# A blocked transpose on VectorE in the inverse of a gated delta rule, and a start that normalizes x tile by tile

## What is computed

```python
h = rmsnorm(x, attn_norm[i])
proj = h @ w_in[i]
qa, ka, va, qb, kb, vb, zb, bb, ab, gl = jnp.split(proj, cuts, axis=-1)
...
# gated delta rule, chunks of 64 tokens
A = jnp.eye(C) + jnp.where(strict, kkT * decay, 0.0)
sol = lax.linalg.triangular_solve(A, rhs, left_side=True, lower=True, unit_diagonal=True)
```

## Time and profile before

| what | value |
|---|---|
| median of 3 runs | 1338.13 us (1337.78 to 1340.0) |
| profiled execution | 1338.62 us |
| its span, first to last instruction | 1336.6 us |
| TensorE busy, share of the span | 1269.8 us, 95% |
| VectorE | 705.7 us, 53% |
| ScalarE | 516.8 us, 39% |
| GpSimd | 634.0 us, 47% |
| time of the first scores, of turn 0, of turn 7 | 62.35, 121.93, about 628 us |

### The profile page before, as it was taken

How to read it: one execution, slowest core, us unless ns; L and a number is a source line. 1 busy time by engine, 2 the same in 40 slices (tenths; PEclk the granted TensorE clock), 3 DMA queues, 4 the chain that set the end, 5 groups by cost and what they waited for, 6 DMA issues and landing times.

```text
span 1336.6 us, 21408 instructions
## 1 busy us (share of the span) xinstructions
PE 1269.8 (95%) x7509; PEld 989.0 (74%) x7509; DVE 705.7 (53%) x1154; ACT 516.8 (39%) x819; POOL 634.0 (47%) x757
## 2 busy tenths in 40 slices
PE   4889999999999999999999999999999999999998
PEld 3657777777777776776788888878887778888776
DVE  3353738475564748376522123118888852871633
ACT  4343544545354544546314222452422122222252
POOL 2433343342434343332544646347666784575543
PEclk9989999999999999999999999999999999999999
DMA  6412111121211111120222435223333242333222
GB/s 186 116 44 63 49 48 49 48 59 38 64 47 49 49 51 46 48 64 21 60 70 73 111 90 168 72 64 92 97 95 94 83 121 80 94 84 104 62 78 82
DMA packets 188136, 100.64 MB, mean 75 GB/s; under 512 B 3654, under 2 KB 186905, under 8 KB 188057
## 3 DMA queue, kind: packets, MB, share of 16 engines
q1 hardware_dynamic: 188057, 99.59, 26.3%
HBM read 97.47 MB, written 2.11 MB: 75 GB/s over the span
## 4 chain that ended last, share of the span: by engine, by line
PE 45%; POOL 20%; issue 18%; DVE 9%; ACT 5%; SPq 1%; DMA 0%; POOLq 0%; DVEq 0%; ACTq 0%
PE bank L496 30%; POOL w_lo L432 20%; PE bank L607 1%; PE bank L692 1%; PE bank L617 1%; PE bank L573 1%; PE bank L593 1%; PE bank L696 1%; PE bank L680 1%; DVE ast L1336 1%; ACT silu L986 1%; DVE qb L1362 1%; ACT silu L987 1%; ACT pr L968 1%; DVE o_b L1417 1%
## 5 line engine op out<-in xcount | busy, mean ns | idle before, releaser
L432 POOL TENSOR_TENSOR w_lo<-w_raw,w_hi 128x256 fp32r<-128x256 f32 x692 | 569.4, 856 | 303.2 <-ACT w_hi L895 298.3
L496 PE MATMUL bank<-hn_hi,w_hi 128*128 128x512 f32 x1000 | 425.3, 425 | 9.8 <-POOL w_lo L432 9.7
L496 PE MATMUL bank<-hn_hi,w_lo 128*128 128x512 f32 x1000 | 393.8, 394 | 0.0
L496 PE MATMUL bank<-hn_lo,w_hi 128*128 128x512 f32 x1000 | 393.0, 393 | 0.0
L446 POOL CAST w_hi<-w_raw 128x1024 fp32r<-128x1024 f32 x61 | 64.4, 1056 | 382.9 <-PE bank L496 382.9
L496 PEld LDWEIGHTS bank<-hn_hi,w_hi 128*128 128x128 f32 x1000 | 189.5, 190 | 61.6 <-issue 19.6
L496 PEld LDWEIGHTS bank<-hn_hi,w_lo 128*128 128x128 f32 x1000 | 189.1, 189 | 41.2
L496 PEld LDWEIGHTS bank<-hn_lo,w_hi 128*128 128x128 f32 x1000 | 190.0, 190 | 38.0 <-issue 6.7
L895 ACT ACTIVATE w_hi<-w_raw 128x1024 fp32r<-128x1024 f32 x120 | 127.5, 1062 | 109.5 <-PE bank L496 95.5
L1197 ACT ACTIVATE s<-u 128x512 f32<-128x512 f32 x22 | 13.9, 634 | 178.4 <-DVEq L1633 178.4
L1630 DVE SCALAR_TENSOR_TENSOR u<-vr,pt,u 128x511 f32<-128x511 f32 x88 | 74.8, 850 | 12.9 <-DVE u L1628 1.2
(11 more groups left out here) (269 smaller groups left out, 1861.8 us busy)
## 6 DMA issues: line engine op xcount, KB each, us to landing
w_raw<-in_w_in SPq DMA_DIRECT2D x73, 512.0 KB, 3.8
w_raw<-in_w_up SPq DMA_DIRECT2D x44, 512.0 KB, 3.8
w_raw<-in_w_down SPq DMA_DIRECT2D x16, 512.0 KB, 3.9
w_raw<-in_w_br_a SPq DMA_DIRECT2D x8, 512.0 KB, 3.8
w_raw<-in_w_br_b SPq DMA_DIRECT2D x8, 512.0 KB, 4.0
w_raw<-in_w_out SPq DMA_DIRECT2D x8, 512.0 KB, 4.1
w_raw<-in_w_ple_gate SPq DMA_DIRECT2D x8, 512.0 KB, 4.0
w_raw<-in_w_down SPq DMA_DIRECT2D x8, 384.0 KB, 3.5
```

The source lines that it names most:

```text
L432: ins = pool.tensor_tensor(wlo[c.slot][:, ks, :], raw[c.slot][:, ks, :], whi[c.slot][:, ks, :].bitcast(F32), ALU.subtract)
L496: mm = pe.matmul(acc, w[c.slot][:, i, :], xx[:, x0 + i, :], start=(i == 0 and n == 0), stop=last)
```

## The change

In the turns, VectorE makes `xi` after level 0, and `xt` after the levels 1 to 4, by transposing the other one in blocks of 32x32 in place (an instruction of VectorE). Up to level 4 all blocks of X off the 32x32 diagonal are zero, so this equals the full transpose. The product at line 657 and the third product of the levels 1 to 4 go, and `level_vt` is signalled by the second product there. Level 5 keeps its third product, level 6 is as it was.

At the start, ScalarE's queue issues the 13 parameter loads; SP's queue issues x, constants, the ba weight, the two loads for the bias line, the qa weight, three small loads, ka and va, and the lead turn's weights after `slope`. Each tile of x gets its own logarithm, exponential and scaling; TensorE transposes six channel blocks tile by tile into six banks, then the last two. TensorE's bias products move ahead of qa, the sums of squares of qa and ka one chunk earlier each. All high halves of the early weights are made by GpSimd. `STEPS_LEAD` changes, with four steps ahead of the first scores.

```diff
-STEPS_LEAD = ((8, 1, 1, 1, 2), (1,) * 6, (1, 1, 1, 1, 1, 1), (2, (1, 1), (1, 1), (1, 1), (1, 1)), (4, 6))
+STEPS_LEAD = (4, (5, 1, 1, 1, 2), (2, 1, 3, 2, 2, 2), (2, 0, 2, 0, 2, 0), (2, (1, 1), (1, 1), (1, 1), (1, 1)), (0, 1))
...
-        IN_BANKS = (3, 4, 5, 1, 2)
+        IN_BANKS = (3, 4, 5, 1, 2, 7)
...
@@ sync @@
-            for plane, row, src in rows:
-                sp.dma_start(prow[row:row + src.shape[0], plane, :], src).then_inc(sem("params_in"), 16)
...
+            load(stream.ba.at(0), w_in0, COLS["ba"])
+            sp.dma_start(hot[:, :], consts[0:33, C_HOT * P:]).then_inc(sem("lines_in"), 16)
+            sp.dma_start(tab[0:32, :], rel_bias).then_inc(sem("lines_in"), 16)
+            load(stream.first.at(0), w_in0, COLS["qa"])
...
+            for n, name in enumerate(("ka", "va")):
+                load(stream.first.at(1 + n), w_in0, COLS[name])
             sp.wait_ge(sem("line_ready"), 1)
...
+            for n, name in enumerate(LEAD):
+                load(stream.lead.at(n), w_in0, COLS[name] + (AHEAD[name] - 1) * P)
@@ gpsimd @@
-            for c in [stream.ba.at(0)] + [stream.first.at(n) for n in range(3)] + [stream.lead.at(n) for n in range(3)]:
-                split(c)
-            for n in range(3, 6):
-                both(stream.lead.at(n))
+            for c in [stream.ba.at(0)] + [stream.first.at(n) for n in range(3)] + [stream.lead.at(n) for n in range(6)]:
+                both(c)
@@ tensor @@
-            pe.wait_ge(sem("small_in"), 16 * 5)
...
+            pe.wait_ge(sem("lines_in"), 16 * 2)
+            pe.wait_ge(sem("tab_set"), 1)
             pe.matmul(bank[6][0:H, 0:LINE], tab[:, :], hot[:, :], start=True, stop=True).then_inc(sem("line_mm"), 1)
...
+            pe.wait_ge(sem("pt_ready"), 1)
+            for t in range(NT):
+                pe.wait_ge(sem("x_normed"), t + 1)
+                for c in range(len(IN_BANKS)):
+                    mm = pe.transpose(bank[IN_BANKS[c]][:, t * P:(t + 1) * P], x_tok[:, t, c * P:(c + 1) * P], ident)
...
             run(gemm(stream.ba.at(0), hn_hi, hn_lo, ready=("h_split", 0)))
-            run(gemm(stream.first.at(0), hn_hi, hn_lo), gemm(stream.first.at(1), hn_hi, hn_lo))
...
             pe.wait_ge(sem("slope_in"), 16)
...
+            run(gemm(stream.first.at(0), hn_hi, hn_lo))
...
+            run(gemm(stream.first.at(1), hn_hi, hn_lo))
...
+            qk_sum(0, 0, stream.first.at(0))
             run(gemm(stream.first.at(2), hn_hi, hn_lo))
+            qk_sum(0, 1, stream.first.at(1))
...
-                if delta:
-                    pe.wait_ge(sem("ct"), h * (NL - 1) + 1)
-                    for t in range(NT):
-                        for q in (LOW, UP):
-                            mm = pe.matmul(packed(7, 0, t, q), ct[0][q, t, :], ident2[q, :], start=True, stop=True)
-                    mm.then_inc(sem("c1"), 1)
...
                         for t in range(NT if n < NL - 1 else 0):
                             for q in (LOW, UP):
-                                pe.matmul(packed(5, 0, t, q), xt[q, t, :], ui[q, t, :], start=True, stop=True)
-                        for t in range(NT):
+                                mm = pe.matmul(packed(5, 0, t, q), xt[q, t, :], ui[q, t, :], start=True, stop=True)
+                        for t in range(NT if n >= NL - 2 else 0):
@@ scalar @@
+            for plane, row, src in rows:
+                act.dma_start(prow[row:row + src.shape[0], plane, :], src).then_inc(sem("params_in"), 16)
...
+                done(nc.scalar.activation(lnx[:, t:t + 1], ss0[:, t:t + 1], ACT.Ln, bias=sm[:, 28:29], scale=1.0 / D),
+                     "x_ln", t + 1)
+                done(nc.scalar.activation(rs0[:, t:t + 1], lnx[:, t:t + 1], ACT.Exp, scale=-0.5), "x_r", t + 1)
...
-                if c == 4:
-                    high(stream.ba.at(0))
...
@@ vector @@
+            def scaled(t):
+                dve.wait_ge(sem("x_r"), t + 1)
                 done(V.tensor_scalar(x_tok[:, t, :], x_tok[:, t, :], rs0[:, t:t + 1], None, ALU.mult), "x_normed", t + 1)
+
+            scaled(0)
+            scaled(1)
             dve.wait_ge(sem("params_T"), 1)
...
             done(V.tensor_copy(line[:, :], bank[6][0:H, 0:LINE]), "line_ready", 1)
+            scaled(2)
+            scaled(3)
...
+                    done(V.transpose(flat(xi), flat(xt)), "xi", h * (NL - 1) + 1)
                 if attention:
                     combine(a, 0)
                 if delta:
-                    dve.wait_ge(sem("c1"), h + 1)
-                    done(V.tensor_tensor(xi[:, :, :], ident2.unsqueeze(1).to_broadcast([P, NT, HEAD]), packed(7),
-                                         ALU.subtract), "xi", h * (NL - 1) + 1)
...
-                            done(V.tensor_tensor(xt[:, :, :], xt[:, :, :], packed(5, 1), ALU.subtract),
-                                 "xt", h * NL + (n + 1))
+                            if n < NL - 2:
+                                done(V.transpose(flat(xt), flat(xi)), "xt", h * NL + (n + 1))
+                            else:
+                                done(V.tensor_tensor(xt[:, :, :], xt[:, :, :], packed(5, 1), ALU.subtract),
+                                     "xt", h * NL + (n + 1))
```

More of the change, by code:

```diff
@@ L373, in _ @@
             sp.dma_start(slope[:, :, :], skew).then_inc(sem("slope_in"), 16)
-            for n, name in enumerate(LEAD[3:]):
-                load(stream.lead.at(3 + n), w_in0, COLS[name] + (AHEAD[name] - 1) * P)
+            for n, name in enumerate(LEAD):
+                load(stream.lead.at(n), w_in0, COLS[name] + (AHEAD[name] - 1) * P)
             for h in range(H - 2):
@@ L562, in _, with qk_sum @@
                           start=True, stop=True).then_inc(sem("bias_mm"), 1)
+            run(gemm(stream.first.at(0), hn_hi, hn_lo))
+            pe.wait_ge(sem("ba_copied"), 1)
+            for t in range(NT):
+                mm = pe.transpose(bank[5][:, t * 16:t * 16 + 16], ba_sb[:, t * P:(t + 1) * P], ident[0:16, 0:16])
+            mm.then_inc(sem("ba_T"), 1)
+            run(gemm(stream.first.at(1), hn_hi, hn_lo))
+            def qk_sum(h, n, c):
+                pe.wait_ge(sem("a_sq"), h * 2 + (n + 1))
+                pe.matmul(bank[c.bank][:, :], half, sqr[n][:, :], start=True, stop=True).then_inc(sem("a_sum"), 1)
+            qk_sum(0, 0, stream.first.at(0))
             run(gemm(stream.first.at(2), hn_hi, hn_lo))
+            qk_sum(0, 1, stream.first.at(1))
             pe.wait_ge(sem("g_ready"), 1)
@@ L568, in _ @@
             pe.matmul(bank[5][:, 96:128], ones, gg, start=True, stop=True).then_inc(sem("g_sums"), 1)
-            def qk_sum(h, n, c):
-                pe.wait_ge(sem("a_sq"), h * 2 + (n + 1))
-                pe.matmul(bank[c.bank][:, :], half, sqr[n][:, :], start=True, stop=True).then_inc(sem("a_sum"), 1)
             def v_turn(h):
@@ L631, in turn @@
                 f = Fill(*fill)
-                early, first, second, scan, late = steps
+                early, first, second, scan, late = steps[-5:]
+                if len(steps) > 5:
+                    f.step(steps[0])
                 if attention:
@@ L938, in v_copy @@
                 done(nc.scalar.activation(va[:, :], bank[4][:, :], ACT.Copy), "va_ready", h + 1)
-            for c in (stream.first.at(0), stream.first.at(1), stream.first.at(2)):
-                high(c)
+            act.wait_ge(sem("lam_sum"), 1)
+            done(nc.scalar.activation(lam_s, lam_s, ACT.Exp), "lam_exp", 1)
+            done(nc.scalar.activation(alexp, alog[:, :], ACT.Exp), "a_exp0", 1)
             prep_qk(0, 0, stream.first.at(0))
-            high(stream.lead.at(0))
             def plane(n):
@@ L952, in _ @@
             prep_qk(0, 1, stream.first.at(1))
-            high(stream.lead.at(1))
+            prep_r(0, 0, stream.first.at(0))
             prep_v(0, stream.first.at(2))
-            high(stream.lead.at(2))
             act.wait_ge(sem("g_cum"), 1)
@@ L1292, in _ @@
             dve.sem_inc(bank_free[c.bank], 1)
+            for n in range(H // 2):
+                bias_copy(n)
             dve.wait_ge(sem("ba_T"), 1)
@@ L1298, in _ @@
                                  dtb[:, :].unsqueeze(1).to_broadcast([P, NT, H]), ALU.add), "ba_planes", 2)
-            for n in range(H // 2):
-                dve.wait_ge(sem("bias_mm"), n + 1)
-                done(V.tensor_copy(bias[:, 2 * n:2 * n + 2, :].rearrange("p a b -> p (a b)"), bank[6 + n % 2][:, :]),
-                     "bias_ready", n + 1)
             dve.wait_ge(sem("soft"), 3)
```

77 lines of the change are left out of this document (28 added, 49 removed).

## The result

The change takes the time from 1338.5 us (1337.78 to 1340.0, 4 runs) to 1307.09 us (1306.03 to 1308.72, 4 runs): ratio 0.9765, 95% interval 0.9748 to 0.9782. Forecast was 1303, range 1294 to 1316. The profiled execution took 1306.31, its span is 1304.5, so 32.1 less than the span of before.

The account below looks back on a forecast made before the run. TensorE, busy 95%, was taken as the bound, shared with VectorE between the first and fifth xi of a middle turn. Gains of 20 us before turn 0 and 14.9 in the turns took 1338.1 to 1303 us, range 1294 to 1316.

Parts of the forecast that it names:

- TensorE's share, 2.79 per turn: Inverse levels on TensorE alone: removed products save 0.71 plus 4 x 0.52, 2.79 us per turn, 22.3 for 8 turns.
- The transpose, 0.42: VectorE in the inverse levels: each 128x256 transpose takes 0.42 us, like the update it replaces; 0.3 and 0.84 kept as alternatives.
- Rival 3: VectorE's transpose in the levels costs 0.84 us, middle turns gain 1.0 instead of 1.8: 1309 us, chance 0.11.
- rival 4: Slower: a very long VectorE transpose delays operations queued behind it, deciding from 1.7 us; at 2.0, 1348 us; chance 0.03.
- Middle turns, 1.8 each: Turns 0 to 5: 1.27 us up to level 4's product plus 0.52 after it, 1.8 each, 10.8 in all.
- rival 1: VectorE has more room, contended rows could relax, turns gain TensorE's whole share of 22.3 us: 1296 us, chance 0.12.
- Turn 0, 1.8: First full turn after the lead turn, counted among turns 0 to 5 as gaining 1.8 us like a middle turn.
- Turn 6, 1.3: Turn without filling in the second half of its levels: gains VectorE's 1.23 us, say 1.3.
- Nothing downstream gives it back: After the turns, from 700 us on, TensorE does matrix products back to back, so the turns' 14.9 us stay gained.
- The start, 20: Everything before turn 0: first scores at 51.5, turn 0 at 101.5 instead of 121.93 us, 20.4 gained, taken as 20.
- Rival 2: Start gains only 10 to 12 us: bias line and slope late on SP's queue, or ba slow-clocked; 1312 us, chance 0.20.
- The lead turn, 50: Turn before turn 0: 43.6 us of work, 5.5 idle and 1 for the clock, 50 in place of 59.58.

Follow-up runs that it names:

- the inverse part alone: Kernel before with only the blocked transposes in place of the inverse levels' products, its start, weights and step lists unchanged: 1322.53 us, ratio 0.9883.
- the start alone: Kernel after with the product behind level 0 and the third products put back, new start and lead-turn list kept: 1320.89 us, ratio 0.9871.
- the identity product back: Kernel after with the ident2 product after level 0 and the xi update from its bank restored in place of the first transpose: 1313.51 us, ratio 0.9814.
- gate and norm later: Kernel after with the previous head's o_b and following VectorE operations moved from behind the third side step to behind the seventh: 1304.89 us, ratio 0.9748.

## Why the prediction held, and where its terms were off

**What bounds the kernel, and the mechanism: right.** VectorE's unbroken stream between the first and the third `xi` passes on what TensorE saves ahead of it and swallows what TensorE saves beside it. Doubling the transposes and putting one product back each moved the time as that picture says.

**TensorE's share, 2.79 per turn: right.** Turn 7, the only one with VectorE nearly free, gained 2.69.

**The transpose, 0.42: measured 0.445.** Rival 3's 0.84 and rival 4's 1.7 are out. From the two-byte figure of the Trainium skill ("VectorE: DVE Perf Modes", "The three transpose paths") the forecast had worked out an estimate of 0.44; the trace agrees with it, for a four-byte tile of 128x256.

**Middle turns, 1.8 each: measured 2.2; the wait, 1.3: measured 0.78.** The term that was off is that the third product's removal doesn't shorten VectorE's stream, and it was put at nothing. The first `xi` of turn 1 came forward by 1.26 counted from the scores (1.23 forecast), but from there to the third `xi` VectorE took 11.04 in place of 11.51. The 0.47 are almost all `o_b`: 0.87 in place of 1.38. This is where GpSimd's copy stands in the three kernels (start and duration), with `o_b` under it; before, after, doubled transposes:

```profile
293.38 1.04 POOL L446 CAST w_hi<-w_raw 128x1024 fp32r<-128x1024 f32 x1 [6.65 <-PE bank L496]
293.59 1.38 DVE L1417 TENSOR_TENSOR o_b<-o_b,sqo 128x512 f32<-128x512 f32 x1
```

```profile
197.25 1.04 POOL L428 CAST w_hi<-w_raw 128x1024 fp32r<-128x1024 f32 x1 [5.71 <-PE bank L476]
197.96 0.87 DVE L1412 TENSOR_TENSOR o_b<-o_b,sqo 128x512 f32<-128x512 f32 x1
```

```profile
198.36 1.04 POOL L428 CAST w_hi<-w_raw 128x1024 fp32r<-128x1024 f32 x1 [5.70 <-PE bank L476]
200.03 0.73 DVE L1412 TENSOR_TENSOR o_b<-o_b,sqo 128x512 f32<-128x512 f32 x1
```

In the first two `o_b` ends 0.69, its undisturbed duration, after a moment 0.14 or 0.15 ahead of the copy's recorded end; in the third the copy was over. The Trainium skill ("SBUF — State Buffer", "SBUF: two separate sides") says that VectorE's operations with two SBUF inputs and GpSimd's share a port pair that one of them holds for its whole instruction while the other stands still. The trace agrees here: 1.38 and 0.87 are "wait, then 0.69". It was not tested by an experiment of its own; the three starts above are what shows it. Forward 1.26, plus 0.47, plus the fourth third product's 0.52, is 2.25 against 2.2 measured. The forecast named this as rival 1's "for" and then kept the contended duration as a constant.

**Turn 0, 1.8: measured 3.8.** The window of before:

```profile
121.93:196.86 74.93, 73.25 (x562) 54.93 (x562) 43.40 (x87) 33.94 (x66) 26.75 (x34) 0.98 0.17 46
```

A granted clock of 0.98, where turn 1 has 1.00: behind a wait of 1.77 at its first scores, filling matmuls took 0.63 from 123.8 to 126.4. After, that wait is 0.26 and the clock 1.00. The two experiments split it: with the inverse part alone turn 0 takes 72.74, 2.2 less, like every middle turn; with the start alone 73.31, 1.6 less. So 1.6 us that this turn gained belong to the start and its clock. The forecast had counted turn 0 as one more middle turn and had nothing for this: a gain by luck, which hides part of the start's shortfall.

**Turn 6, 1.3: measured 0.** VectorE's first `xi` of the levels came 1.25 earlier, as forecast. Then the contention that eased the middle turns went the other way: the product with `silu` met GpSimd's subtraction, and only 0.80 of the 1.25 reached the product of level 4. In before and in after:

```profile
595.11 0.69 DVE L1377 TENSOR_TENSOR qb<-qb,silu 128x512 f32<-128x512 f32 x1
```

```profile
563.12 1.10 DVE L1372 TENSOR_TENSOR qb<-qb,silu 128x512 f32<-128x512 f32 x1
...
570.19 0.42 DVE L1455 TENSOR_TENSOR xi<-xi,bank 128x256 f32<-128x256 f32 x1 [1.17 <-PE bank L670]
```

TensorE's wait grew from 1.7 to 2.78, and the lower clock behind it took the 0.80: VectorE's next `xi` waited 1.17 for TensorE, where it had waited for nothing in before, and both kernels pass the second sum of squares within 0.04 of each other, counted from the scores. The forecast had no term for the clock behind a longer wait. Moving filling there gave 3.6 back.

**Nothing downstream gives back: not quite.** 1.4 came back between 945 and 1211, where TensorE waits for GpSimd's low halves 8.6 us in 11 waits against 7.4 in 10. The stretch before and after:

```profile
979.09:1243.14 264.05, 256.67 (x1122) 208.77 (x1120) 168.64 (x209) 61.73 (x65) 173.81 (x191) 1.00 0.33 94
```

```profile
945.55:1211.06 265.51, 256.90 (x1121) 208.81 (x1120) 168.89 (x209) 61.65 (x65) 174.21 (x191) 1.00 0.32 93
```

The code there is the same in all kernels. Between the same two products it takes 264.0 with the start alone, with doubled transposes and with the identity product back, 264.8 with the inverse alone, and 265.4 to 265.5 in after and the eight other runs. So neither part of the change alone brings the 1.4. What makes one or the other come stays open.

**The start, 20: measured 16.** First scores at 54.36, not 51.5; 2.3 of the 2.9 are ba's end (27.3, not 25). Step by step: the two loads for the bias line landed at 13.1 as assumed (13). The two tiles behind the line copy took 2.28, not 1.6, beside GpSimd's early halves (1.54 with GpSimd idle), and ended at 17.55, not 16.6. From there to the first high half of x are 1.4, for which the forecast had 0.4: TensorE's 24 transposes go tile by tile and end at 19.9, not 17. Each of these two steps is 1 us of the error, and the first alone is not worth mending: scaling all tiles by 14.2 left the high half where it was, at 18.85. So the first low half was complete at 20.5 in place of 18.5; eight of them at 0.78 is the forecast's pace. Of the assumption "the weight is in no one's way" two things failed: the weight's halves slow VectorE's scaling, and left to ScalarE they would have cost 5.5. Rival 2's mechanisms did not come: the line was out at 15.26, `slope` issued at 18.47, and the bias products at 27.32 did not wait; and the ba product ran at the upper clock level.

**ScalarE's queue.** The forecast gave the ScalarE queue 4.5 of issue time as a cost and took SP's relief for granted. With the loads back on SP's queue the time is the same, so neither mattered. The Trainium skill ("DMA: Bandwidth & Descriptors", "Issuing engines are not separate DMA queues") says that DMAs share the 16 engines whoever starts them; the trace agrees, landings moved by 0.3 where issues moved by 1.8 to 2.4.

**The lead turn, 50: measured 51.53.** The forecast was 49 and 1 for the clock. At a granted clock of 1.00 the same list takes 49.96 (VectorE scales first) or 49.97 (high halves by ScalarE); in after it is 0.97, so the list took 1 more than forecast and the clock cost 1.6, not 1, in this execution. What remains of the softmax wait is 2.55, forecast 2; the second sum of squares, which lost its cover, waits 2.1.

In the sum the errors went both ways: start and lead turn 4 short, turns 1 to 5 2 more, turn 0 2 more, turn 6 1.3 short, downstream 1.4 short. The mechanisms of the main case were right, and its time was 4 off. Without the gains at `o_b` and at turn 0's clock, which nothing in the forecast stood for, it would have been 8 off, still inside the range: that part of the closeness is luck.

## What to carry to other kernels

Where two engines share a bound, split a saving by its place: what the bounding stream waits for counts in full, what runs beside it counts nothing until that stream is shorter. Look at what stands ahead of a short operation that the busiest engine needs: one operation moved behind it gave 9.3 us, a third of what the whole change gave. And when a wait moves, price the clock behind it too.

## What the runs showed of the hardware

- A transpose of VectorE in 32x32 blocks, four-byte, 128x256, SBUF to SBUF: 0.445 us, 40 times alike.
- TensorE's clock: behind waits of 2.78 (turn 6 of after), 2.10 (turn 6 with gate and norm later) and 4.51 (high halves by ScalarE) matmuls of 512 columns took 0.63 in place of 0.39 for some microseconds. Behind the waits of 0.78, of 1.38 in every scan, and of 1.69 in turn 6 of before, none did.
- The length of the wait alone doesn't tell. Twelve of the kernels wait 2.5 to 2.6 for the third softmax of the lead turn. In nine the granted clock behind it was 0.74 over 6.5 us; in two it was 1.00, and these are the lead turns of 49.96 and 49.97 in place of 51.5. The wait of 2.1 at the end of that turn was followed by the lower level in three of the twelve, and one of 1.77 at its end in before was.
- Executions of one kernel differ in this too. After itself took 1306.31 and 1306.03 at a mean granted clock of 0.997, 1307.86 and 1308.72 at 0.994. The same wait of 2.0 near the end of the program was followed by a lower clock in four of the fourteen profiled executions, and their last stretch takes 95.1 in place of 93.4.
- An operation of VectorE with two SBUF inputs beside GpSimd's copy: 1.38 or 0.87 in place of 0.69, by where it starts. Two scalings of 128x1024 beside GpSimd's subtraction: 2.28 in place of 1.54.
- 13 DMA issues by ScalarE take from 0.85 to 5.79, beside the table load of 1.28.
